# Sums of squares: pair adds on GpSimd ahead of the ones-matmuls, and the context's sum one step later

## What is computed

```
def _rmsnorm(x, g):
    xf = x.astype(jnp.float32)
    y = xf * lax.rsqrt(jnp.mean(xf * xf, axis=-1, keepdims=True) + EPS)
    return (y * g.astype(jnp.float32)).astype(x.dtype)
```

## Time and profile before

| | us |
|---|---|
| median of 3 runs | 1423.33 |
| lowest, highest | 1423.07, 1425.75 |
| the profiled execution | 1427.52 |
| its span in the trace | 1425.7 |
| TensorE busy (share of the span) | 1368.6 (96%) |
| VectorE, ScalarE, GpSimd busy | 848.8 (60%), 746.8 (52%), 108.5 (8%) |

### The profile page before, as it was taken

The page is one execution under the profiler, slowest core; times in us unless marked ns, Lnnn a source line. Parts: engine busy times, 40 slices in busy tenths (PEclk is TensorE's granted clock), DMA queues, the critical chain, the costliest instruction groups (busy, mean ns, idle before and its releaser), DMA issues.

```text
span 1425.7 us, 24918 instructions
## 1 busy us (share of the span) xinstructions
PE 1368.6 (96%) x10484; PEld 1239.8 (87%) x10484; DVE 848.8 (60%) x1283; ACT 746.8 (52%) x1209; POOL 108.5 (8%) x65
## 2 busy tenths in 40 slices
PE   5999899998999999998999999999999999998998
PEld 2989788998999998997899998999897778687978
DVE  3557765556688876478665476544474535428654
ACT  3565465664645544565666545554554564326562
POOL 0000000101000000000000110000003433121000
PEclk8999999999999999999999999999999999999999
DMA  9955566455799995642844467875452222032430
GB/s 342 375 171 182 183 231 237 129 197 189 239 321 373 353 370 165 219 144 78 290 148 145 157 202 273 298 243 178 157 157 89 71 78 89 30 98 89 133 105 30
DMA packets 194722, 269.54 MB, mean 189 GB/s; under 512 B 5037, under 2 KB 174386, under 8 KB 188338
## 3 DMA queue, kind: packets, MB, share of 16 engines
q1 hardware_dynamic: 194610, 267.94, 56.4%
HBM read 266.87 MB, written 1.05 MB: 188 GB/s over the span
## 4 chain that ended last, share of the span: by engine, by line
PE 80%; DVE 11%; ACT 5%; issue 2%; SPq 1%; DMA 1%; DVEq 0%; ACTq 0%
PE first_dense L1653 13%; PE first_dense L1657 13%; PE first_dense L1655 13%; PE first_dense L991 5%; PE first_dense L994 5%; PE first_dense L993 5%; DVE first_w_lo L539 2%; PE first_misc L238 2%; PE first_dense L1821 2%; PE first_s L1653 2%; PE first_s L1657 2%; PE first_s L1655 2%; ACT first_w_hi L533 1%; DMA first_units<-in_w_ada 1%; PE first_o L1657 1%
## 5 line engine op out<-in xcount | busy, mean ns | idle before, releaser
L539 DVE TENSOR_TENSOR first_w_lo<-first_raw,first_w_hi 128x1024 fp32r<-128x1024 f32 (+2 forms) x304 | 366.5, 1217 | 280.8 <-ACT first_w_hi L533 279.7
L533 ACT ACTIVATE first_w_hi<-first_raw 128x1024 fp32r<-128x1024 f32 (+2 forms) x304 | 313.8, 1041 | 252.9 <-PE first_dense L1657 99.3
L1653 PE MATMUL first_dense<-first_h_parts,first_w_hi 128*128 128x256 f32 x1312 | 374.4, 285 | 3.4 <-DVE first_h_parts L2278 3.4
L1655 PE MATMUL first_dense<-first_h_parts,first_w_hi 128*128 128x256 f32 x1312 | 371.2, 283 | 0.0
L1657 PE MATMUL first_dense<-first_h_parts,first_w_lo 128*128 128x256 f32 x1312 | 371.1, 283 | 0.0
L1653 PEld LDWEIGHTS first_dense<-first_h_parts,first_w_hi 128*128 128x128 f32 x1312 | 251.5, 192 | 13.9 <-issue 9.8
L1655 PEld LDWEIGHTS first_dense<-first_h_parts,first_w_hi 128*128 128x128 f32 x1312 | 251.6, 192 | 0.1
L1657 PEld LDWEIGHTS first_dense<-first_h_parts,first_w_lo 128*128 128x128 f32 x1312 | 251.6, 192 | 0.0
L993 PE MATMUL first_dense<-first_parts,first_w_hi 128*128 128x512 f32 (+1 forms) x400 | 137.0, 342 | 0.0
L991 PE MATMUL first_dense<-first_h_parts,first_w_hi 128*128 128x512 f32 (+1 forms) x336 | 118.1, 352 | 0.9 <-DVE first_w_lo L685 0.9
L994 PE MATMUL first_dense<-first_h_parts,first_w_lo 128*128 128x512 f32 (+1 forms) x336 | 115.6, 344 | 0.0
(11 more groups left out here) (393 smaller groups left out, 2657.2 us busy)
## 6 DMA issues: line engine op xcount, KB each, us to landing
first_raw<-in_w_in SPq DMA_DIRECT2D x78, 1024.0 KB, 5.5
first_raw<-in_w_ff SPq DMA_DIRECT2D x64, 1024.0 KB, 7.0
first_units<-in_w_ada SPq DMA_DIRECT2D x34, 1024.0 KB, 6.5
first_units<-in_w_mod SPq DMA_DIRECT2D x17, 1024.0 KB, 6.8
first_raw<-in_w_out SPq DMA_DIRECT2D x16, 1024.0 KB, 5.0
first_mb<-in_w_ada SPq DMA_DIRECT2D x10, 1024.0 KB, 7.8
first_mb<-in_w_mod SPq DMA_DIRECT2D x7, 1024.0 KB, 7.2
first_raw<-in_w_uq SPq DMA_DIRECT2D x6, 768.0 KB, 4.5
```

The source lines that it names most:

```text
L533: act.activation(w_hi[g % SPLIT][:, c], raw[g % CHUNK_RING][:, c], ACT.Copy).then_inc(hi_made, 1)
L539: dve.tensor_tensor(w_lo[g % SPLIT][:, c], raw[g % CHUNK_RING][:, c], w_hi[g % SPLIT][:, c].bitcast(F32), ALU.subtract).then_inc(lo_made, 1)
L1653: pe.matmul(out, still[0](t), moving[0](t), start=start and t == n == 0, stop=False, skip_group_check=True)
L1655: pe.matmul(out, still[0](t), moving[1](t), start=False, stop=False, skip_group_check=True)
```

## The change

Three sums are made differently; the sum with weights and the ones-sum of x at step 31 stay as they are.

1. The context's squares: GpSimd adds pairs 1, 2 and 3 onto pair 0 (`turn_pool`, step 25, three additions of 128x512). TensorE makes 2 ones-matmuls in place of 8, and makes them behind the chunk of step 27 and not ahead of the chunk of step 26.
2. The squares between the second block's layers: GpSimd adds pairs 1 and 2 of each stream onto pair 0 (four additions of 128x512), from the place of the last out unit in its order. TensorE makes all its ones-matmuls at the end, 4 for each stream (tiles 0, 1, 6, 7) and so 8 in place of 16; those between the out units are gone.

```
-        CTX_TURN, CTX_SUM, CTX_NORM, CTX_LOW = 24, 26, 27, 29
+        CTX_TURN, CTX_SUM, CTX_NORM, CTX_LOW = 24, 27, 27, 29
...
+        def turn_tensor_behind(pe, step):
+
             if step == CTX_SUM:
                 pe.wait_ge(ctx_copied, 4)
-                for t in range(KT):
-                    if t % 2 == 0:
-                        pe.wait_ge(ctx_squared, t // 2 + 1)
-                    last = pe.matmul(ctx_ssq, ones, ctx_sq[:, t, :], start=t == 0, stop=t == KT - 1)
+                pe.wait_ge(ctx_added, 3)
+                for t in range(2):
+                    last = pe.matmul(ctx_ssq, ones, ctx_sq[:, t, :], start=t == 0, stop=t == 1)
                 last.then_inc(ctx_summed, 1)
...
+        def turn_pool(pool, step):
+            if step == CTX_TURN + 1:
+                for i in (1, 2, 3):
+                    pool.wait_ge(ctx_squared, i + 1)
+                    if i > 1:
+                        pool.wait_ge(ctx_added, i - 1)
+                    pool.tensor_tensor(ctx_sq[:, 0:2, :], ctx_sq[:, 0:2, :], ctx_sq[:, 2 * i:2 * i + 2, :], ALU.add).then_inc(
+                        ctx_added, 1)
...
-                def next_squares(pairs, streams):
-
-                    for s in streams:
-                        for i in pairs:
-                            pe.wait_ge(before["next_squared"], SEQ2 * i + s + 1)
-                            for t in (2 * i, 2 * i + 1):
-                                last = pe.matmul((misc, t_bank[1])[s][:, 0:S], ones, sq2[s][:, t, :], start=t == 0,
-                                                 stop=t == KT - 1)
-                        if pairs[-1] == KT // 2 - 1:
-                            last.then_inc(before["next_summed"], 1)
+                def next_squares():
+
+                    for s in range(SEQ2):
+                        pe.wait_ge(next_added, 2 * SEQ2)
+                        for t in (0, 1, 6, 7):
+                            if t == 6:
+                                pe.wait_ge(before["next_squared"], SEQ2 * 3 + s + 1)
+                            last = pe.matmul((misc, t_bank[1])[s][:, 0:S], ones, sq2[s][:, t, :], start=t == 0, stop=t == 7)
+                        last.then_inc(before["next_summed"], 1)
...
-                    pair = out_pair(n)
-                    if pair is not None and ctx_out and 2 <= pair:
-
-                        next_squares((pair - 2,), range(SEQ2))
...
-                    next_squares((2, 3), range(SEQ2))
+                    next_squares()
...
+                    if ctx_out and out_pair(n) == 3:
+                        for i in (1, 2):
+                            for s in range(SEQ2):
+                                pool.wait_ge(before["next_squared"], SEQ2 * i + s + 1)
+                                if i == 2:
+                                    pool.wait_ge(next_added, s + 1)
+                                pool.tensor_tensor(sq2[s][:, 0:2, :], sq2[s][:, 0:2, :], sq2[s][:, 2 * i:2 * i + 2, :],
+                                                   ALU.add).then_inc(next_added, 1)
```

6 lines of the change are left out of this document (4 added, 2 removed).

## The result

The changed kernel takes 1415.62 us, the median of 4 runs (1415.26 to 1415.92), against 1423.72 us (1423.07 to 1425.75) of the kernel before on the same chip. The ratio is 0.9938, with a 95% interval of 0.9922 to 0.9954. It is 8.1 us faster; forecast were 9.0 us and 1414.3. The profiled execution has a span of 1414.1 us for 1425.7.

The account below looks back on a forecast made before the run. TensorE, busy 96% of the span, was taken as the bound. Terms 6.60 + 1.73 + 0.70 = 9.03 us gave 1423.33 - 9.03 = 1414.3 us; the 8-in-10 range was 1412.5 to 1418.0.

Parts of the forecast that it names:

- The place at step 26: Context's sum: 7.46 us removed at step 26, 0.86 added behind step 27, net 6.60 us; 4.85 at full clock.
- The additions: GpSimd's three context additions, at 1.81 us each, end 3.5 us before TensorE asks; the four between layers have 7 us.
- a lead of 6.05 us at step 28: VectorE's low part for step 28 ends 6.05 us before it is needed, so its product does not wait.
- The rule against the change: GpSimd and two-input VectorE operations share ports under an exclusive lock, so a low part meeting an addition waits for all of it.
- Behind out pair 2: Between the second block's layers, four sum matmuls behind out pair 2 go: 1.73 us, all on TensorE's path.
- The end of the layer: Second block's first layer: 4 of 12 sum matmuls go, but TensorE waits about 1.0 us for pair 3's square; 0.70 us gained.
- My first rival: Executions without a profile keep full clock at step 26's sum: 7.28 us saved in all, 1416.1 us; chance 0.25.
- The carry-over of the 4.2 us: The profiled execution lay 4.2 us above the runs' median; the forecast carried this difference over to the changed kernel.
- Nothing between the layers: Clock falls behind the waits at the layer's end, costing 1.5 us or all 2.43: 1416.7, or 1418.5 with both rivals; 0.12.
- my sign of being wrong: Wrong if TensorE waits for additions, steps 26 to 31 idle for low parts or DMAs, or the clock falls elsewhere.
- GpSimd holding VectorE up: Seven additions of 1.67 us each hold back a low part TensorE waits for: 11.7 us, 1426.0 us; chance 0.04.
- the sums to stay on the path: Late additions make TensorE wait at step 27, or the norm delays step 28's splits: 1419 to 1423 us; chance 0.07.

Follow-up runs that it names:

- The kernel with the other order: Changed kernel with the last sum matmuls reordered: tiles 0 and 1 of x and context, then 6 and 7 of both; 1416.80 us.
- the one with the early square: Changed kernel, but ScalarE squares x's last pair right behind its residual and splits the second half of its weights behind both squares; 1418.44 us.
- both halves: Kernel before with only the context's part of the change, 1418.15 us; and with only the part between the second block's layers, 1422.54 us.
- the move alone: Kernel before with all eight context ones-matmuls moved behind step 27, no additions on GpSimd, layers as before; 1422.84 us.
- the one with eight unused matmuls: Kernel before with eight 128-column matmuls, result unread, ahead of the wait for the context's squares at step 26; 1423.14 us.
- the context's half alone: Kernel before with only the context's part: three GpSimd additions, two matmuls behind step 27, between the layers as before; 1418.15 us.
- the kernel with all four waits filled: Changed kernel with unused matmuls in four TensorE waits, the first block's 12 and 16 ahead of the fourth pair of heads; 1414.43 us.

## Why the prediction was right, and where a size was off

**The place at step 26.** Forecast 6.60 us, and 4.85 where the clock stays up; measured 6.60 and 4.92, by the distances above. Its parts held: 0.86 us for the two matmuls behind step 27, none for the wait ahead of them, none for ScalarE's norm.

**The additions.** Forecast: they end 3.5 us before TensorE asks for them; it was 3.8. Their sizes differ from the 1.81 us that I took: two took 1.29 and 1.30, and only the one under a low part 2.10. The low parts themselves took 0.64 and 0.43 us longer, which I had priced only in the rival. It cost nothing: no dense product waits for them. The prediction had a lead of 6.05 us at step 28; here the low part of 1025.51 ends at 1027.38, 5.66 us ahead of that step's first product. Between the layers the four additions end at 1269.81, and TensorE asks for them at 1275.72. The margin is 5.9 us and not 7: I had let pair 2's squares come 1.73 us earlier with the sum ahead of them gone, but ScalarE did not wait for that sum.

**The rule against the change.** The rows agree with it now in both orders. The low part of 1025.51 meets an addition that has 0.79 us left and takes 0.64 longer; the addition of 1026.44 meets this low part with 0.94 us left and takes 0.81 longer than the 1.29 of the first; the low part of 1027.96 meets this addition with 0.58 us left and takes 0.43 longer. That is what the Trainium skill, SBUF — State Buffer, section "SBUF: two separate sides", states: who comes second waits for the other to end. The price is here some 0.14 us less than the rest of one instruction, not its full length, and it fell on instructions with lead.

**Behind out pair 2.** Forecast 1.73 us, measured 1.76 (12.88 - 11.12).

**The end of the layer.** Forecast 0.70 us, measured 0.59; here a term was mis-sized. The wait was right: tiles 6 and 7 start 1.89 us after the sum's start in both. But I let them give the slot away 0.86 us later, by 2 x 0.43, and it took 0.97 (1277.61 to 1278.58). The first matmul behind a wait costs about 0.1 us more; the row of the other norm shows it, 1.13 us for four records against 1.02. ScalarE starts the norm 3.06 us after the sum's start for 3.65, which is the 0.59. The kernel with the other order shows that the context's sum does not set the restart; the one with the early square shows that VectorE's last low part is close behind x's chain.

**The median.** The sum of the measured terms is 8.95 us where the clock had fallen at step 26 and 7.27 where not. The three measurements of the change gave 8.1, 7.0 and 5.7 us (1423.18 - 1417.49). Only the first lies where a mixture of both should; the other two are below it, with intervals of 5.1 to 8.7 and 4.4 to 8.0 us that reach into it. With a fall in three of four executions (the estimate above) the terms give 8.5 us. That the forecast of 9.0 came so near to the first measurement is in part luck; what the medians lack to the terms stays open. My first rival, full clock at step 26 in some executions, is thus partly true; I had given it 0.25 as a case of its own and should have made it a share of the executions. The carry-over of the 4.2 us by which the profiled execution lay above the median held: behind 1380, at 551 and in the first 160 us the executions differ by the clock's falls, in kernels with the change and without it. One thing stays open: the fall behind 1380 is in the trace of before, in those of both halves and of the move, but in none of the three of the changed kernel. The kernel with the other order has it, so the change does not rule it out.

**The other rivals.** Nothing between the layers: the clock did fall in the next layer's start, as it said, in the changed kernel:

```profile
1284.00:1286.00 2.00, 2.00 (x11) 2.00 (x11) 1.93 (x6) 1.47 (x4) 0.00 (x0) 0.50 0.00 0
```

So my sign of being wrong, a fall elsewhere, was there. But the kernel before has the same idle time of 2.35 us there, and two kernels with the old sums between the layers showed that fall too, the move alone at 1288 to 1291 and the one with eight unused matmuls at 1291 to 1294. It costs next to nothing, where I had said 1.5 us: from the restart to the next unit of 512 columns it is 1298.38 - 1282.82 = 15.56 us here and 15.54 in the context's half alone, which had no fall. Behind these products TensorE waits for VectorE anyway, 0.87 to 0.89 us in executions without the fall and not at all in this one. GpSimd holding VectorE up did not come; for the sums to stay on the path it took six more additions.

## What to carry to other kernels

A sum that a tensor engine makes in the middle of its products costs its wait first and its matmuls second: moving it past the products of two steps (from ahead of 26 to behind 27) gave 2.3 to 4.0 us of the 4.9 to 6.6, before any work was taken away. Check the lead of every operand in the new place by starts and ends in the timeline, and at a wait between layers look for the operation with which the chain begins, since work removed ahead of it turns into waiting. Before filling a wait or moving work into it, find the place by counting the trace's rows, size the filling from the moment at which its own buffer comes free, and look at what TensorE waits for next: a late low part can swallow most of what the clock gives back.

## What the runs showed of the hardware

TensorE's granted clock fell to half (1.2 for 2.4 GHz) behind idle times of 2.10, 2.34 and 2.35 us in some executions and not in others of the same instructions. At 551 the changed kernel has the fall in one of its three traces and not in the others, behind the same 2.34 us; the first takes 1.47 us more from there to the next wait at 663 (113.28 for 111.81). At step 26 the fall cost 1.68 us, behind 1380 about 1.6, at 1284 nothing. Behind 4.01 us of idle time at 663 the clock stayed down for 6.8 us in the changed kernel's traces, and that cost only 0.6 to 0.8 us, since VectorE's low parts end the stretch. Eight to sixteen unused matmuls kept the clock up in each wait that they filled; at 155 and 663 all twelve traces with the full waits have the fall. Single falls like these, at places that change from run to run, are of the size of the scatter of both kernels (1421.2 to 1427.4 us in all runs of before but two, 1415.3 to 1418.4 after). That they are its cause is made likely, not shown: the kernel with all four waits filled still scatters by 2.5 us. A part lies ahead of all four: with the same instructions up to there TensorE comes out of the wait at 155 at 153.67 us in one trace and at 155.70 in another.
